# Expert gates from two fp32r terms instead of three bf16 terms, and all low parts of the down units on GpSimd

## What is computed

```python
s = jnp.einsum("thpd,hpnd->thpn", q, keys)          # two halves of 128 keys, 8 heads
s1, i1 = lax.top_k(s[:, :, 0], 16); s2, i2 = lax.top_k(s[:, :, 1], 16)
comb = s1[..., :, None] + s2[..., None, :]
sc, ci = lax.top_k(comb.reshape(...), 16)
e1, e2 = take(i1, ci // 16), take(i2, ci % 16)
gate = softmax(sc)
pre = einsum("td,thkd->thk", xt, down[e1 * 128 + e2])
out = einsum("thk,thkd->td", gelu(pre) * gate, up[e1 * 128 + e2])
```

## Time and profile before

| | us |
|---|---|
| median of three executions (3241.45 to 3241.85) | 3241.63 |
| the profiled execution, its own time | 3241.09 |
| its span | 3239.3 |
| PE busy in the span | 2957.5 |
| DVE busy | 1832.0 |
| ACT busy | 1071.3 |
| POOL busy | 524.2 |

### The profile page before, as it was taken

One profiled execution on the slowest core, in us unless ns is written; L12 is line 12 of the kernel. 1 busy time (PEld: TensorE's weight loads), 2 busy tenths in 40 slices (PEclk: granted clock), 3 DMA queues, 4 the chain that ended last, 5 costly groups with the idle time before them and its releaser, 6 DMA issues.

```text
span 3239.3 us, 54519 instructions
## 1 busy us (share of the span) xinstructions
PE 2957.5 (91%) x20890; PEld 2722.8 (84%) x20890; DVE 1832.0 (57%) x2953; ACT 1071.3 (33%) x1744; POOL 524.2 (16%) x220
## 2 busy tenths in 40 slices
PE   7897867989999999999998978589899999999998
PEld 5687655878899999999976866558789999999997
DVE  1742585217956676666627317752199466666665
ACT  1211121004543334555502112200155443355554
POOL 0000010005862220000000000200078522300000
PEclk9996776999999999999998958769999999999999
DMA  5210310333553335555451103113245433355553
GB/s 188 79 66 27 109 65 30 130 117 109 158 160 120 122 119 162 180 181 179 156 185 66 66 14 114 60 43 143 91 137 162 150 123 122 118 174 177 181 181 123
DMA packets 113036, 395.78 MB, mean 122 GB/s; under 512 B 17122, under 2 KB 18658, under 8 KB 111780
## 3 DMA queue, kind: packets, MB, share of 16 engines
q1 hardware_dynamic: 105124, 379.18, 35.7%
q10 hardware_dynamic: 7808, 15.21, 1.6%
HBM read 385.44 MB, written 8.53 MB: 122 GB/s over the span
## 4 chain that ended last, share of the span: by engine, by line
PE 60%; issue 21%; POOL 8%; DVE 8%; ACT 1%; DMA 0%; ACTq 0%; POOLq 0%; SPq 0%; DVEq 0%
PE bank L414 59%; POOL WHL L1679 7%; DVE arena L1171 5%; POOL arena L1675 1%; ACT arena L872 1%; DVE arena L1269 0%; PE bank L565 0%; DMA arena<-arena 0%; DVE hT L1179 0%; ACT L872 0%; DVE arena L1353 0%; DVE arena L1360 0%; PE bank L607 0%; DVE arena L1175 0%; ACTq L966 0%
## 5 line engine op out<-in xcount | busy, mean ns | idle before, releaser
L414 PE MATMUL bank<-HHL,WHL 128*128 128x264 f32 x6144 | 796.4, 288 | 26.8 <-POOL WHL L1679 21.2
L414 PEld LDWEIGHTS bank<-HHL,WHL 128*128 128x128 f32 x6144 | 763.8, 190 | 37.3 <-POOL WHL L1679 28.4
L414 PE MATMUL bank<-AHL,WHL 128*128 128x264 f32 x6144 | 747.9, 284 | 0.0
L414 PEld LDWEIGHTS bank<-AHL,WHL 128*128 128x128 f32 x6144 | 747.7, 188 | 0.0
L872 ACT ACTIVATE WHL<-raw 128x1024 fp32r<-128x1024 f32 x512 | 542.4, 1060 | 335.3 <-PE bank L414 333.7
L1679 POOL TENSOR_TENSOR WHL<-raw,WHL 128x1024 fp32r<-128x1024 f32 x188 | 485.2, 2587 | 1006.0 <-ACT WHL L872 1006.0
L414 PE MATMUL bank<-hT,ring 128*128 128x264 f32 (+1 forms) x2496 | 588.6, 397 | 19.6 <-DVE hT L1179 11.7
L414 PEld LDWEIGHTS bank<-hT,ring 128*128 128x128 f32 x2496 | 481.6, 194 | 114.8 <-DVE hT L1179 12.5
L414 PE MATMUL bank<-arena 64*64 64x64 f32 (+7 forms) x3200 | 352.7, 280 | 123.0 <-DVE arena L1171 112.6
L414 PEld LDWEIGHTS bank<-arena 64*64 64x64 f32 (+3 forms) x3200 | 319.5, 187 | 164.8 <-DVE arena L1171 108.1
L1171 DVE TENSOR_TENSOR arena<-arena 128x128 f32<-128x128 f32 (+5 forms) x422 | 289.2, 727 | 227.4 <-ACT arena L872 145.6
(11 more groups left out here) (108 smaller groups left out, 1485.2 us busy)
## 6 DMA issues: line engine op xcount, KB each, us to landing
raw<-down SPq DMA_DIRECT2D x256, 512.0 KB, 3.5
raw<-up SPq DMA_DIRECT2D x256, 512.0 KB, 3.5
ring<-wm SPq DMA_DIRECT2D x100, 1024.0 KB, 4.9
arena<-hs ACTq DMA_DIRECT2D x2, 1280.0 KB, 7.7
o_hs<-arena ACTq DMA_DIRECT2D x2, 1280.0 KB, 4.5
arena<-cm SPq DMA_DIRECT2D x2, 1160.0 KB
arena<-rs ACTq DMA_DIRECT2D x2, 1024.0 KB, 7.6
o_rs<-arena ACTq DMA_DIRECT2D x2, 1024.0 KB, 6.8
```

Source lines behind the costliest of these rows:

```text
L414: return pe.matmul(out, lhsT, rhs, start=start, stop=stop)
```

## The change

- Gate values are split into two fp32r terms (`GP`) instead of three bf16 ones, so a token's gates are two matmuls of 128 x 128, a block's are 8 instead of 12, with fp32r operands on both sides. Their four tokens are still interleaved: the column stride of the operands was 8 bytes and is 16 bytes.
- `one_hot` becomes three DVE instructions: the second key's one-hot in bf16 (`OHK`, a view of `NRM`, one buffer), the first key's in fp32r (`OHE`), and the product in fp32r (`OHG`, 2 x 512 elements). It waits for its own previous product (`oh_ready`).
- POOL makes the low parts of all 128 down units; DVE only those of the up units. SP and PE wait for `plo_done` accordingly.
- `GT` moves from SBUF to PSUM banks 4 and 5. The first up unit of a layer writes those banks from its third output on, so PE waits there for the last `gated_later` (`ev_done`).
- `HHL`, `GP` and the one-hots change places in SBUF; the arena of the mixer is larger. Two DVE steps that made the third term, and a subtraction, are gone.

```diff
-NODD = (NK - GU) // 2
-NPOOL = GU + NODD
+NPOOL = NK
...
-        GP = sb("GP", P, 3, T, dt=BF16)
-        OHE = sb("OHE", P, GB, 2, NK, TB, dt=BF16)
-        OHG = sb("OHG", P, GB, 3, NK, TB, dt=BF16)
-        GT = sb("GT", P, 2, T)
+        GP = sb("GP", P, 2, T, dt=FR)
+        OHE = sb("OHE", P, GB, NK, TB, dt=FR)
+        OHK = NRM[:, 0:NK * TB // 2].bitcast(BF16).rearrange("p (e t) -> p e t", t=TB)
+        OHG = sb("OHG", P, GB, 2, NK, TB, dt=FR)
+        GT = bank[4:6]
...
                     for t in range(TB):
-                        for q in range(3):
-                            ins = mm(bank[6 + b][:, t * NK:(t + 1) * NK], OHE[:, b, 0, :, t],
-                                     OHG[:, b, q, :, t], q == 0, q == 2)
+                        for q in range(2):
+                            ins = mm(bank[6 + b][:, t * NK:(t + 1) * NK], OHE[:, b, :, t],
+                                     OHG[:, b, q, :, t], q == 0, q == 1)
...
                     for k in range(4):
+                        if begin and v == 0 and k == 2:
+                            pe.wait_ge(S["ev_done"], (l + 1) * (NK - GU))
                         for j in range(2):
...
-                    ins = tt(RES[:, tcc], bank[2 + tc][:, 2 * P:2 * P + m], GP[:, 0, tcc], ALU.subtract)
-                step(ins)
-                step(dve.tensor_copy(GP[:, 1], RES))
-                step(tt(RES, RES, GP[:, 1], ALU.subtract))
-                done(dve.tensor_copy(GP[:, 2], RES), "et_evac", l + 1)
+                    ins = tt(GP[:, 1, tcc], bank[2 + tc][:, 2 * P:2 * P + m], GP[:, 0, tcc].bitcast(F32), ALU.subtract)
+                done(ins, "et_evac", l + 1)
...
-                    keys = ET[:, :, tok].rearrange("p k (a t) -> p k a t", a=1).broadcast_to([P, 2, NK, TB])
-                    iota = IOTA[:].rearrange("p (a e) t -> p a e t", a=1).broadcast_to([P, 2, NK, TB])
-                    tt(OHE[:, b], keys, iota, ALU.is_equal).then_inc(S["oe_ready"], 1)
-                    dve.wait_ge(S["oe_ready"], l * NB + s + 1)
-                    both = OHE[:, b, 1].rearrange("p (q e) t -> p q e t", q=1).broadcast_to([P, 3, NK, TB])
-                    tt(OHG[:, b], both, rows4(GP[:, :, tok], NK), ALU.mult).then_inc(S["oh_ready"], 1)
+                    dve.wait_ge(S["oh_ready"], l * NB + s)
+                    for k, out in ((1, OHK), (0, OHE[:, b])):
+                        tt(out, rows(ET[:, k, tok], NK), IOTA[:], ALU.is_equal).then_inc(S["oe_ready"], 1)
+                    dve.wait_ge(S["oe_ready"], 2 * (l * NB + s) + 1)
+                    both = OHK.rearrange("p (q e) t -> p q e t", q=1).broadcast_to([P, 2, NK, TB])
+                    tt(OHG[:, b], both, rows4(GP[:, :, tok].bitcast(F32), NK), ALU.mult).then_inc(S["oh_ready"], 1)
...
-                low(GU, 0, 0, 0)
                 one_hot(0)
...
-                    if n % 2:
-                        low(n + 1, (n + 1) % 2, (n + 1) % 4, 0)
                     gated(s)
...
-                with pool.Fori(0, GU // SLOTS) as i:
+                with pool.Fori(0, NK // SLOTS) as i:
                     for b in range(SLOTS):
                         low(b, b % 2, b, i * SLOTS)
-                with pool.Fori(0, NODD // 2) as i:
-                    for b in (1, 3):
-                        low(GU + b, 1, b, i * SLOTS)
```

More of the change, by code:

```diff
@@ L130, in build @@
         ctx.enter_context(pair_memory)
-        ARENA = 36240
+        ARENA = 40336
         mixer_memory = ExitStack()
@@ L231, in build @@
         ACTS = sb("ACTS", P, NK, T)
+        HHL = sb("HHL", P, 2, KD, T, dt=FR)
         ET = sb("ET", P, 2, T, dt=BF16)
-        GP = sb("GP", P, 3, T, dt=BF16)
-        OHE = sb("OHE", P, GB, 2, NK, TB, dt=BF16)
-        OHG = sb("OHG", P, GB, 3, NK, TB, dt=BF16)
-        GT = sb("GT", P, 2, T)
+        GP = sb("GP", P, 2, T, dt=FR)
[3 more added lines that the diff above has]
+        GT = bank[4:6]
         IOTA = sb("IOTA", P, NK, TB, dt=BF16)
-        sb("gap", P, 488)
+        sb("gap", P, 248)
         WHL = sb("WHL", P, 2, 2, D_MODEL, dt=FR)
         raw = sb("raw", P, SLOTS, D_MODEL)
-        HHL = sb("HHL", P, 2, KD, T, dt=FR)
         TKN = 14400
@@ L378, in up @@
                 def up(v, slot, turn):
-                    sp.wait_ge(S["vlo_done"], turn + (l * NVEC + NODD + v - SLOTS + 1))
+                    sp.wait_ge(S["vlo_done"], turn + (l * NVEC + v - SLOTS + 1))
                     sp.dma_start(raw[:, slot], d["up"][l][bass.ds(turn + v, 1)].rearrange("a p m -> p (a m)"))\
@@ L387, in _ @@
                     down(slot, slot, 0)
-                with sp.Fori(0, GU // SLOTS) as i:
+                with sp.Fori(0, NK // SLOTS - 1) as i:
                     for b in range(SLOTS):
@@ L391, in _ @@
                         down(SLOTS + b, b, i * SLOTS)
[L392 to L398, removed]
                 for b in range(SLOTS):
[L400 to L403, removed]
+                    sp.wait_ge(S["plo_done"], (l + 1) * NPOOL - SLOTS + b + 1)
                     sp.dma_start(raw[:, b], d["up"][l][b]).then_inc(raw_in[b], 16)
@@ L772, in gates, with down @@
                     for t in range(TB):
-                        for q in range(3):
-                            ins = mm(bank[6 + b][:, t * NK:(t + 1) * NK], OHE[:, b, 0, :, t],
-                                     OHG[:, b, q, :, t], q == 0, q == 2)
+                        for q in range(2):
+                            ins = mm(bank[6 + b][:, t * NK:(t + 1) * NK], OHE[:, b, :, t],
+                                     OHG[:, b, q, :, t], q == 0, q == 1)
                     ins.then_inc(S["g_mm"], 1)
                 def low_part(u, turn):
-                    if u < GU:
+                    if u < NK:
                         pe.wait_ge(S["plo_done"], turn + (l * NPOOL + u + 1))
[L782 to L785, removed]
-                    else:
-                        pe.wait_ge(S["vlo_done"], turn + (l * NVEC + (u - GU) // 2 + 1))
-                def down(n, b, turn, between=None, pair=None):
+                    else:
+                        pe.wait_ge(S["vlo_done"], turn + (l * NVEC + u - NK + 1))
+                def down(n, b, turn, between=None):
                     pe.wait_ge(S["gelu_done"], turn + (l * NK + n + 1))
@@ L797, in down @@
                         between()
-                    low_part(n, turn if pair is None else pair)
+                    low_part(n, turn)
                     for k in range(KD):
@@ L841, in _ @@
                     for b in range(2):
-                        down(GU + b, b, i * 2, lambda: gates(l * NB + b, b, i * 2), i)
+                        down(GU + b, b, i * 2, lambda: gates(l * NB + b, b, i * 2))
                 for n in range(GU + NB, NK):
@@ L1098, in gelu_gated @@
                         act.wait_ge(S["ev_done"], l * (NK - GU) + n - GU - 1)
-                    ins = f(GT[:, n % 2, 0:tokens], bank[n % 2][:, 0:tokens], ACT.Gelu)
+                    ins = f(GT[n % 2][:, 0:tokens], bank[n % 2][:, 0:tokens], ACT.Gelu)
                     if tokens < T:
@@ L1602, in gated_later @@
                     a = ACTS[:, n, 0:tokens]
-                    tt(a, a, GT[:, n % 2, 0:tokens], ALU.mult).then_inc(S["ev_done"], 1)
+                    tt(a, a, GT[n % 2][:, 0:tokens], ALU.mult).then_inc(S["ev_done"], 1)
                 def low(u, b, slot, turn):
```

## The result

The changed kernel takes 3304.6 us (3304.5 to 3307.8, four executions) against 3241.7 us (3241.4 to 3242.3, four): 1.0194 of the time before, 95% interval 1.0182 to 1.0207, or 63 us more. The forecast was 3234 us with a range to 3300: wrong in direction and outside the range.

What follows compares the result with a forecast made beforehand. PE bounds the blocks before; after the change the port shared by DVE and POOL, 4.27 us a block. -9.5 - 3 + 3.8 + 1 = -7.7 us on 3241.1 gives 3233.4, the median 0.5 above: 3234 us, range 3226 to 3300.

Steps and rivals of the forecast that it cites:

- The gate matmul, 0.125 us: Blocks, on PE: each of 8 fp32r gate matmuls costs 0.125 us, the price of the 264-column fp32r row.
- the term of PE's block: Blocks: PE's own work per block, 8 gate matmuls (1.00 us) plus the unit's 3.00 us, 4.00 us.
- The first rival: Blocks: gate matmul slow at 128 columns, 0.233 us each, PE's block 4.86 us, kernel 3316 us; chance 0.27.
- the price does not matter up to 0.159: Blocks: a gate matmul of up to 0.159 us keeps PE's block within the 4.27 us that bounds it.
- The port, 4.27 us: Blocks: two-SBUF-input DVE instructions and POOL low parts exclude each other; block 4.342 to 4.27 us, -9.5 us.
- The lead, -3 us: First blocks of a layer: PE's pace until POOL's and DVE's lead is used up, 1.5 us a layer.
- Ahead of the first block, +1: Before a layer's first block: one-hots beside POOL's low parts put these off, 0.5 us a layer, +1 us.
- The first up unit, 1.9 us a layer: First up unit: PE waits after four matmuls for the last `gated_later`, 1.9 us a layer, +3.8 us.
- this price (1.7): After the first up unit's wait: a lowered clock would cost at most 1.7 us a layer more; none taken.
- SP, `GT` in PSUM, the removed steps: `raw` loads, gelu written to PSUM, and the third term's removed DVE steps: each changes the time by nothing.

Runs made afterwards that it cites:

- both_contig: Changed kernel with both operands of the gate matmuls stored token by token, columns adjacent instead of 16 bytes apart: 3232.2 us.
- weights_contig: Changed kernel with only the gate matmuls' weights (`OHE`) stored token by token, the moving operand still at 16 bytes: 3234.1 us.
- split_lows: Changed kernel with its fp32r gates, but low parts shared between DVE (even units) and POOL (odd units) as before the change: 3304.6 us.
- bf16_gates: Changed kernel with its gates undone (three bf16 terms, 12 matmuls a block), POOL still making every low part: 3248.7 us.

## Why the prediction was wrong, step by step

- **The gate matmul, 0.125 us: the step that failed.** It is 0.2335, from the load of strided weights; the term of PE's block was 4.00 us and is 4.77. The first rival named the 16 bytes among its reasons and had 0.233, 4.86 us and 3316 us (the block is 4.77, since the gates take 1.82 and not 1.86 us and the unit 2.95 and not 3.00); I gave it 0.27. That its price fits is luck: it was taken from the plain fp32 matmul of this width, two records of 0.116 on contiguous columns, and the width that it blamed costs nothing (0.112 in `both_contig`). The row held against it, the plain fp32 record at 0.116, has contiguous weights: it is a price for the type and the width, and says nothing of the stride. Nor did the 264-column row. The forecast's sentence that the price does not matter up to 0.159 was right, and with 0.118 `weights_contig` took 3234.1 us, where 3234 was forecast. That the tenth agrees is luck too: against the trace before, its blocks and hand-overs gained 10.7 us and not 7.7, and what lies outside them took 3.7 us more.
- The Trainium skill's lines of 16 bytes with two hits ("SBUF — State Buffer", "Door 1: The DMA port swizzle") fit the fp32r weights: 193 and 196 ns with four and two columns in 16 bytes, 328 with one. They do not fit the moving operand (0.006 us) nor, in size, the bf16 weights with one column in 16 bytes (29 ns), and the same note's free stride of four fp32 does not hold for weights.
- **The port, 4.27 us: right, though hidden in the changed kernel**, where PE's 4.77 lies above it. In `weights_contig` it was 4.26, turn by turn. `OHK`, `OHE` and `OHG` cost 0.42, 0.69 and 1.22 us where nothing held them, against 0.41, 0.68 and 1.22.
- **The lead, -3 us: right in size, and not to be had.** Blocks at 4.77 us leave none to use. In `weights_contig` the first four blocks of a layer took 3.87 us instead of 4.26: 1.6 us a layer, where I had 1.5.
- **Ahead of the first block, +1: it cost nothing.** There `OHK`, `OHE` and `OHG` stretched to 2.44, 2.88 and 3.43 us beside the low parts, but from the first down unit to the first gates it took 0.2 to 0.3 us less than before.
- **The first up unit, 1.9 us a layer: 1.75 us of idle time, a gap of 2.0 between starts.** The up units took 2.4 us longer in layer 0. In layer 1 it was 4.0: fifteen matmuls ran at 0.220 us after the gap, 1.5 us in all, with the granted clock at 0.71 on average over 2905 to 2910, that is partly at 1.2 GHz. I had named this price (1.7) and taken none of it. It is no fixed price of the gap: of the 20 layers with this gap in ten traces only three show it, and `split_lows`, with the same gates, in neither layer.
- **SP, `GT` in PSUM, the removed steps: nothing, as forecast.** A gelu into PSUM took 0.37 us for 264 tokens.
- **The range** ended at 0.22 us for a gate matmul, just under the 0.233 of the first rival. Where a rival is a step from one price to another, the range either holds it or does not.

## What to carry to other kernels

A price from another row holds only if the access pattern is the same too: before an operand becomes wider in place, look at the distance between its columns, above all of the weights of a matmul, whose load can then set the time. Where four-byte weights would lie 16 bytes apart, let the engine that writes them put the columns side by side; here it cost DVE nothing and was worth some 70 us. When a bound is removed, add up what the next engine has in its own queue, and not only the resource that it shares.

## What the runs showed of the hardware that was not expected

- An fp32r weight load of 128 columns takes 193 ns contiguous, 196 at 8 bytes, 328 at 16; the starts of the matmuls go from 0.118 to 0.2335 us. The bf16 load takes 118 ns at 8 bytes and 147 at 16. A moving operand of 128 fp32r columns at 16 bytes costs 0.006 us more than a contiguous one.
- A gap of 2.0 us on PE between full stretches was followed by about fifteen matmuls at nearly half the rate (0.220 us instead of 0.122) in three of 20 layers: one of the changed kernel, both of `bf16_gates`, and none of the eight other runs that have the gap. What decides it stays open.
- DVE instructions with one fp32 tensor in SBUF and scalars per partition exclude a GpSimd low part: eight of them took 6.26 us beside two low parts and 2.13 alone, a single one 2.41 instead of 0.34.
